# Two fused blocks on one core: a second feed-forward of seven products, with the order of its high parts and weight sums changed and its streamed weights begun earlier

## What is computed

```python
def mlp(s, shift, scale_m):
    hm = rms_norm_2(s, g_norm2) * (1.0 + scale_m) + shift
    return jnp.square(jax.nn.relu(hm @ w_mlp1)) @ w_mlp2
x_new = x_new + gt2 * mlp(x_new, sh2, sc2)
```

## Time and profile before

| | |
|---|---|
| median of 3 runs | 3619.94 us (3619.88 to 3622.87) |
| the profiled execution | 3623.87 us |
| its span | 3622.0 us |
| TensorE busy (PE) | 3371.3 us, 93% |
| VectorE busy (DVE) | 2051.3 us, 57% |
| ScalarE busy (ACT) | 1317.9 us, 36% |
| GpSimd busy (POOL) | 497.4 us, 14% |
| mean granted TensorE clock | 0.967 |

### The profile page before, as it was taken

How to read it: one execution, slowest core, us unless ns; L and a number is a source line. 1 busy time by engine, 2 the same in 40 slices (tenths; PEclk the granted TensorE clock), 3 DMA queues, 4 the chain that set the end, 5 groups by cost and what they waited for, 6 DMA issues and landing times. The chain is left out here.

```text
span 3622.0 us, 49595 instructions
## 1 busy us (share of the span) xinstructions
PE 3371.3 (93%) x19426; PEld 2585.7 (71%) x19426; DVE 2051.3 (57%) x3893; ACT 1317.9 (36%) x2358; POOL 497.4 (14%) x353
## 2 busy tenths in 40 slices
PE   7999999999999999999986676999999999998997
PEld 6767778887888888875555565547888467777876
DVE  4276982233785555336468885569211176666885
ACT  3276761222311111124444553138211044444442
POOL 1190000110101111010000000116001123331000
PEclk9999999999999999999997887999999999999999
DMA  4101111112333333123011214100121214437444
GB/s 138 38 2 38 43 46 50 53 53 82 97 96 95 98 95 102 47 77 131 4 23 35 47 36 117 51 9 2 35 76 58 84 56 148 140 136 274 140 171 154
DMA packets 307426, 287.69 MB, mean 79 GB/s; under 512 B 66964, under 2 KB 249172, under 8 KB 304764
## 3 DMA queue, kind: packets, MB, share of 16 engines
q1 hardware_dynamic: 305436, 277.44, 23.7%
q10 hardware_dynamic: 1760, 7.08, 0.9%
HBM read 227.43 MB, written 55.21 MB: 78 GB/s over the span
## 5 line engine op out<-in xcount | busy, mean ns | idle before, releaser
L95 PE MATMUL ps<-halves 128*128 128x512 f32 x7376 | 1705.5, 392 | 16.5 <-DVE halves L403 5.6
L95 PEld LDWEIGHTS ps<-halves 128*128 128x128 f32 x7376 | 1384.3, 188 | 309.1 <-issue 11.3
L1773 PE MATMUL ps<-halves 128*128 128x512 f32 x1368 | 323.8, 395 | 18.5 <-DVE halves L1730 16.5
L1817 PE MATMUL ps<-halves 128*128 128x512 f32 x1344 | 310.5, 392 | 19.2 <-DVE halves L1730 18.9
L95 PE MATMUL ps<-arena 128*128 128x512 f32 (+1 forms) x800 | 315.2, 554 | 5.8 <-ACT arena L2853 3.0
L1773 PEld LDWEIGHTS ps<-halves 128*128 128x128 f32 x1368 | 255.1, 189 | 87.2 <-issue 33.3
L1817 PEld LDWEIGHTS ps<-halves 128*128 128x128 f32 x1344 | 252.4, 189 | 77.2 <-DVE halves L1730 24.9
L95 PEld LDWEIGHTS ps<-arena 128*128 128x128 f32 x800 | 151.9, 191 | 162.5 <-issue 152.6
L1407 DVE SCALAR_TENSOR_TENSOR arena<-arena,sc 128x128 f32<-128x128 f32 x448 | 164.2, 367 | 15.9
L1563 POOL TENSOR_TENSOR tmps<-tmps 128x512 f32<-128x512 f32 x64 | 73.8, 1152 | 693.3 <-ACT tmps L1531 693.3
L1730 DVE TENSOR_TENSOR halves<-raws,halves 128x512 fp32r<-128x512 f32 x162 | 132.4, 821 | 59.4 <-ACT halves L1726 59.4
(11 more groups left out here) (372 smaller groups left out, 4116.6 us busy)
## 6 DMA issues: line engine op xcount, KB each, us to landing
raws<-in_w_ff SPq DMA_DIRECT2D x31, 1024.0 KB, 6.7
mixw<-in_w_in SPq DMA_DIRECT2D x56, 512.0 KB, 3.9
hidden_rows<-staged SPq DMA_DIRECT2D x16, 1792.0 KB, 5.9
raws<-hidden_rows SPq DMA_DIRECT2D x28, 1024.0 KB, 5.1
arena<-in_w_ada SPq DMA_DIRECT2D x48, 512.0 KB, 3.8
raws<-in_w_mlp SPq DMA_DIRECT2D x32, 512.0 KB, 5.5
arena<-in_w_mlp SPq DMA_DIRECT2D x16, 1024.0 KB, 7.4
arena<-in_w_in SPq DMA_DIRECT2D x5, 2048.0 KB, 11.9
```

The lines of the kernel that those rows point to most:

```text
L95: ins = e.matmul(out_ap, l, r, start=i == 0, stop=i == n - 1)
L1773: ins = e.matmul(o[:, :], l[:, k, :], r[:, k, :], start=first and k == 0 and i == 0, stop=last and k == 3 and i == 2)
L1817: ins = e.matmul(banks[t][:, :], l, r, start=kt == 0 and j == 0, stop=kt == 15 and j == 2)
```

## The change

ScalarE's and VectorE's orders in the steady bodies are written anew. For bodies with a next panel, with x the entry of A11 of panel n + 1, they are (H a high part, L a low part, in the order of the entries):

| | before | after |
|---|---|---|
| ScalarE | relu 12 of n-1; H A11; copy m1; H A12; relu 11; H S2, S3, A22; relu 21; H S1; relu 22; H S4 | H A11, A12; copy m1; H S2; relu 12 of n-1; H S3, A22; relu 11; H S1, S4; relu 21; relu 22 |
| VectorE | upper right of n-1; L A11; S1, S2; L A12; first corner; L S2; S3; joint; L S3; third joint; S4; L A22; lower left; L S1; lower right; L S4 | upper right of n-1; S1, S2; L A11, A12; S3; first corner; L S2; S4; joint; L S3; third joint; L A22; lower left; L S1; lower right; L S4 |

The last body (n = 15), whose entries are the down stage's first, changes too. The first kept piece is loaded as two halves. The streamed pieces get four places, at the addresses of T1's and T2's parts, and a piece for rows(r+2) is issued behind rows(r), the output behind rows(27).

```diff
--- before.py
+++ after.py
@@ -1687,7 +1687,7 @@
         kept = lambda q, kt: KEPT[(0 if q == "B11" else 4) + kt // 4][:, kt % 4 * 512:kt % 4 * 512 + 512]
         down_rows = lambda u: RAW[:, u // 4 % 2 * 2048 + u % 4 * 512:u // 4 % 2 * 2048 + u % 4 * 512 + 512]
         stream_piece = lambda i, kt: 4 * STREAMED.index(i) + kt // 4
-        streamed = lambda i, kt: R(43008 + stream_piece(i, kt) % 2 * 2048 + kt % 4 * 512, 512)
+        streamed = lambda i, kt: R(38912 + kt // 4 * 2048 + kt % 4 * 512, 512)
         down_total = lambda i, kt: DSUM[:, kt % 4 * 512:kt % 4 * 512 + 512]
 
         def down_weights(u):
@@ -1722,7 +1722,7 @@
                 elif i in SUMMED:
                     e.wait_ge(*down_sum(i, kt))
                 else:
-                    e.wait_ge(*kept_there(DOWNW[i][0], kt // 4))
+                    e.wait_ge(*kept_there(DOWNW[i][0], kt // 4, kt % 4))
             e.activation(entry_part(x, 0), entry_source(x), ACT.Copy).then_inc(*f_wh.tick())
 
         def vector_entry(e, x):
@@ -1731,8 +1731,8 @@
                             ALU.subtract).then_inc(*f_ws.tick())
 
         W_BASE = (5, 2, 2, 2)
-        kept_there = lambda q, t: l_w[t].at(W_BASE[t] + (1 if q == "B11" else 2))
-        stream_there = lambda x: l_m[x % 2].at(40 + x // 2 + 1)
+        kept_there = lambda q, t, kt=3: l_m[0].at(41) if (q, t) == ("B11", 0) and kt < 2 else l_w[t].at(W_BASE[t] + (1 if q == "B11" else 2))
+        stream_there = lambda x: l_w[x % 4].at(W_BASE[x % 4] + 2 + x // 4 + 1)
         hidden_out = lambda n: l_h[n % 2].at(n // 2 + 1)
 
         def weight_sum(e, n, s):
@@ -1921,21 +1921,28 @@
             H(22)
             for n in range(2, 16):
                 x = steady_at(n + 1, "A11")
+                more = n < 15
+                H(x)
+                if more:
+                    H(x + 1)
+                scalar_common(e, n)
+                if more:
+                    H(x + 2)
                 scalar_relu(e, n - 1, "12")
-                H(x)
-                scalar_common(e, n)
-                if n < 15:
-                    H(x + 1)
+                if more:
+                    H(x + 3, x + 4)
                 scalar_relu(e, n, "11")
-                if n == 15:
-                    H(x + 1)
-                H(x + 2, x + 3, x + 4)
+                if more:
+                    H(x + 5, x + 6)
+                else:
+                    H(x + 1, x + 2, x + 3)
                 scalar_relu(e, n, "21")
-                H(x + 5)
+                if not more:
+                    H(x + 4, x + 5)
                 scalar_relu(e, n, "22")
-                if n == 15:
+                if not more:
                     scalar_row(e, 1, G2)
-                H(x + 6)
+                    H(x + 6)
             scalar_relu(e, 15, "12")
             H(*range(DOWN0 + 7, DOWN0 + 224))
 
@@ -2040,26 +2047,27 @@
                 x = steady_at(n + 1, "A11")
                 more = n < 15
                 upper_right(n - 1)
-                L(x)
                 if more:
                     weight_sum(e, n + 1, "S1")
                     weight_sum(e, n + 1, "S2")
-                    L(x + 1)
+                    L(x, x + 1)
+                    weight_sum(e, n + 1, "S3")
+                else:
+                    L(x)
                 first_corner(n)
                 if more:
                     L(x + 2)
-                    weight_sum(e, n + 1, "S3")
+                    weight_sum(e, n + 1, "S4")
                 joint(n)
                 L(x + 3 if more else x + 1)
                 third_joint(n)
                 if more:
-                    weight_sum(e, n + 1, "S4")
+                    L(x + 4)
                 else:
                     vector_row(e, 40, TM3)
                     L(x + 2, x + 3)
-                L(x + 4)
                 lower_left(n)
-                L(x + 5)
+                L(*((x + 5,) if more else (x + 4, x + 5)))
                 lower_right(n)
                 L(x + 6)
             upper_right(15)
@@ -2182,17 +2190,22 @@
                 e.wait_ge(*s_done(steady_at(15, free)))
                 if q == "B22":
                     e.wait_ge(*kept_there("B11", t))
-                e.dma_start(KEPT[(0 if q == "B11" else 4) + t][:, :].rearrange("p (k n) -> p k n", k=4),
-                            quad(q, t)).then_inc(*l_w[t].tick())
+                place = KEPT[(0 if q == "B11" else 4) + t][:, :].rearrange("p (k n) -> p k n", k=4)
+                if (q, t) == ("B11", 0):
+                    e.dma_start(place[:, 0:2, :], quad(q, t)[:, 0:2, :]).then_inc(*l_m[0].tick())
+                    e.dma_start(place[:, 2:4, :], quad(q, t)[:, 2:4, :]).then_inc(*l_w[t].tick())
+                else:
+                    e.dma_start(place, quad(q, t)).then_inc(*l_w[t].tick())
 
             def stream(i, t):
                 x = stream_piece(i, 4 * t)
-                if x < 2:
+                if x < 4:
                     e.wait_ge(*bk.full(("row", 1, 1)))
+                    e.wait_ge(*kept_there("B22", t))
                 else:
-                    e.wait_ge(*down_sum(STREAMED[(x - 2) // 4], (x - 2) % 4 * 4 + 3))
-                e.dma_start(R(43008 + x % 2 * 2048, 2048).rearrange("p (k n) -> p k n", k=4),
-                            quad(DOWNW[i][0], t)).then_inc(*l_m[x % 2].tick())
+                    e.wait_ge(*down_sum(STREAMED[(x - 4) // 4], 4 * t + 3))
+                e.dma_start(R(38912 + t * 2048, 2048).rearrange("p (k n) -> p k n", k=4),
+                            quad(DOWNW[i][0], t)).then_inc(*l_w[t].tick())
 
             weights(0)
             weights(1)
@@ -2225,13 +2238,11 @@
                         e.wait_ge(*hidden_out(14 + k))
                     for h in range(2):
                         e.dma_start(X[:, 4 * h:4 * h + 4, :], x_of(xs)[:, 4 * h:4 * h + 4, :]).then_inc(*l_x3[h].tick())
-                i, t = ORDER7[r // 4], r % 4
-                if i in STREAMED:
-                    stream(i, t)
-                if r == 26:
-                    e.wait_ge(*f_ad.at(adds_to(5, len(SCALED[5]) - 1)))
-                    e.dma_start(x_of(out)[:, 4:8, :], X[:, 4:8, :]).then_inc(*l_out.tick())
-                    e.dma_start(x_of(out)[:, 0:4, 512:1024], X[:, 0:4, 512:1024]).then_inc(*l_out.tick())
+                if r < 26 and ORDER7[(r + 2) // 4] in STREAMED:
+                    stream(ORDER7[(r + 2) // 4], (r + 2) % 4)
+            e.wait_ge(*f_ad.at(adds_to(5, len(SCALED[5]) - 1)))
+            e.dma_start(x_of(out)[:, 4:8, :], X[:, 4:8, :]).then_inc(*l_out.tick())
+            e.dma_start(x_of(out)[:, 0:4, 512:1024], X[:, 0:4, 512:1024]).then_inc(*l_out.tick())
             for t in range(4):
                 e.wait_ge(*f_ad.at(adds_to(6, t)))
                 e.dma_start(x_of(out)[:, t, 0:512], X[:, t, 0:512]).then_inc(*l_out.tick())
```

## The result

The changed kernel takes **3563.27 us** (median of 4 runs, 3559.67 to 3566.88) beside 3621.4 us for the kernel before in its 4 runs; the ratio is 0.9836, 95% interval 0.9819 to 0.9853, so 1.6% faster. The profiled execution took 3559.67 us with a span of 3557.9; the forecast for the span was 3559.0 and for the median 3557, with a high end of 3574 and a low end some 5 us under the forecast. The direction, the range and the two stage times held.

What follows compares the result with a forecast made beforehand. ScalarE and VectorE waiting for each other were taken to bound the up stage, late streamed weights to cost the down stage. Gains of 38.3 and 24.7 us sum to 63.0, from 3619.94 to 3557 us; main case 3552 to 3562, high end 3574.

Steps and rivals of the forecast that it cites:

- high end: Whole kernel: 3574 us, taking in two rivals, VectorE's bound (3 us) and the kept piece (7 us) together.
- low end: Whole kernel: takes 5 us of other losses that may vanish, such as earlier half-clock stretches.
- What bounds the kernel: Steady panels: VectorE and ScalarE wait for each other, making bodies 21.4 us where TensorE could take 19.06.
- Up stage: From 3017.53 to 3286.19: 268.7 us falls to 228.7 plus 1.7 for the row product, gaining 38.3 us.
- Down stage: From 3286.19 to 3615.87: 329.7 us falls to 305.0 as waits for streamed weights go, gaining 24.7 us.
- The walk of a body: Steady body, ScalarE's steps timed from S4's end: 12.5 to 14 us without TensorE's pace, 5 us to absorb lateness.
- The bound of 18.8 us: VectorE in a steady panel: 11.8 us unstretched plus all of GpSimd's 7.04 us, still under 19.06.
- the first rival: Steady bodies: VectorE and GpSimd lock each other out, bodies take 19.5 us, 6 us back, 3563; chance 0.12.
- Panel 15: Before the row product: first kept half lands in 5.4 us, diagonal ready by 13 us, no TensorE idle.
- The rival of a late kept piece: Before the row product: TensorE stands and its clock falls, up to 12 us back, 3563 to 3569; chance 0.10.
- The slower rival: Up stage: exchange of waits stays, A11's low part 2.5 us later in 13 bodies, 3628 us; chance 0.03.
- The predicted time: Whole kernel: profiled 3623.87 less 63.0 gives 3560.9, span 3559.0; median taken 3.9 us lower, 3557 us.

Runs made afterwards that it cites:

- e3: The changed kernel with VectorE's old order in the steady bodies, ScalarE's new order and the streaming kept; 3564.76 us, ratio 0.9821 to the kernel before.
- e4: The changed kernel with ScalarE's old order, VectorE's new order kept; 3591.77 us, ratio 0.9897 to the kernel before.
- e1: The changed kernel with only the new ScalarE and VectorE orders: weights streamed as before, first kept piece in one; 3590.13 us, ratio 0.9891 to the kernel before.
- first new start: The changed kernel with panel 0's first corner, third token sums and plain-token copies moved ahead at the up stage's start; 3560.84 us, ratio 0.9818 to the kernel before.

## Why the prediction was right

- **What bounds the kernel.** ScalarE and VectorE waiting for each other: shown, by e3 (opening it on ScalarE's side gives all) and e4 (VectorE's side gives 10.5 us of 38).
- **Up stage: 38.3 us predicted, 38.1 measured.** 84 matmuls at 0.2269 us are 19.06 us, the window has 19.05. The row product took 1.3 us from start to start, for 1.7.
- **Down stage: 24.7 predicted, 24.6 measured.** 305.0 was the forecast and 305.1 the time.
- **The walk of a body.** Its stations fit: A11' high part 0.5 to 1.1 us into the body (1.2), copy of m1 3.6 to 4.1 (3.9). VectorE's share did not: the walk gave 5 us of room, the trace has 3.3. The stretches beside GpSimd grew from a VectorE busy time of 14.16 to 15.72 us a panel; S2 now takes 1.57 us where it took 0.69. In the rows of the body above S1 ends at 3094.89, 0.55 us after GpSimd's instruction that had started before it, and S2 at 3096.59, 0.56 us after the next one: each looks as if it did its work only when GpSimd was through. The rule of the Trainium skill (SBUF — State Buffer, SBUF: two separate sides) says that such a pair locks each other out for a whole instruction; the trace agrees, with two-input additions of 1.57 to 1.78 us beside GpSimd's and 0.68 us alone. The bound of 18.8 us held, and what it cost lay in idle time, so the first rival (bodies of 19.5 us) did not come; that the median equals its 3563 is chance.
- **Panel 15.** The half of the first kept piece landed in 3.5 us, not 5.4, and two halves have a median of 4.3 us; the whole pieces take 11.4:

```profile
kept<-in_w_mlp SPq DMA_DIRECT2D x7, 1024.0 KB, 11.4
...
kept<-in_w_mlp SPq DMA_DIRECT2D x2, 512.0 KB, 4.3
```

  The diagonal was ready at 3239.1, 3 us before TensorE came. The rival of a late kept piece was priced with 13.3 us, the median of pieces issued one behind another. The first of them has none ahead of it: in e1, whole, it landed in 5.1 us, and no idle followed. The split was not needed. Rows(2) was issued 8.2 us after the first down product, not 6, and in time.
- **The slower rival** was mis-priced: 2.5 us a body, where e4 measures a body 0.8 us shorter.
- **The predicted time.** The span was 3559.0 predicted and 3557.9 measured, but the median 3563.27 lies 6 us over 3557. The step that missed is the last: I took the profiled execution of before as 3.9 us slow and subtracted that, where the profiled execution of the changed kernel, 3559.67 us, was the fastest of its four and 3.6 us under their median. In the profiles of this study the first product of the stage starts at 2920.4 (after), 2921.9 (before) and up to 2930.1 us (the changed kernel again), in parts of the kernel that are the same. That spread, and not the change, set the distance.

## What to carry to other kernels

When two engines serve a third in turn and all three have idle time, look at the order of the waits before the sizes of the work: here it was enough to let ScalarE make the next operands before it touched results, up to the limit that a ring of eight entries sets, and VectorE's order was of no account. A transfer's place in the issuing queue, behind a wait or a bulk output, can matter more than how many buffers it has: four places issued late were worth 0.4 us. And before paying for a margin, such as a piece split in two, price it from a transfer with as much ahead of it in the queue: 5.1 us for the first piece, where the median of all was 13.3.

## What the runs showed of the hardware that I had not expected

TensorE's clock fell after idles of 2.3 us. In the steady panels with eight additional additions, idles of 2.26, 2.27 and 0.62 us take turns, and the panel behind the second long one, every third, has a granted clock of 0.92 (84 matmuls in 20.9 us for 19.3), the others 1.00. In the first new start one idle of 2.29 us is followed by 0.79 over the next 8 us (2963.95 to 2972.00). Idles of 1.2 us a panel, in the kernel before and in e4, left it at 1.00. What such a fall costs depends on who sets the pace: nothing in those panels, where VectorE did, and a part of 9.1 us in the last one, where TensorE was the bound.

And the first 2920 us of the same program differed by 10 us between the two profiled executions of the changed kernel (2920.37 and 2930.14 us to the first product), with the last 637 us equal to 0.5 us; stages were therefore the better measure than medians here.
